# The attention phase of a three-layer kernel: the third group's output gate moves behind the fourth group's queries, keys and values

## What is computed

```python
def attention_mixer(h, positions, w_in, b_in, sinks, w_out, b_out):
    proj = h @ w_in + b_in
    q, k, v, z = jnp.split(proj, [ATTN_WIDTH, ATTN_WIDTH + KV_WIDTH, ATTN_WIDTH + 2 * KV_WIDTH], axis=-1)
    q = partial_rope(q.reshape(B, T, N_HEADS, HEAD_DIM), positions)
    k = partial_rope(k.reshape(B, T, N_KV_HEADS, HEAD_DIM), positions)
    o = sliding_window_gqa(q, k, v, sinks)
    return (o * jax.nn.silu(z)) @ w_out + b_out
```

## Time and profile before

| | us |
|---|---|
| median of three runs (3653.46 to 3659.43) | 3657.53 |
| the profiled execution: its time | 3661.34 |
| its span | 3660.0 |
| TensorE busy | 3461.1 (95%) |
| VectorE busy | 2063.2 (56%) |
| ScalarE busy | 1719.2 (47%) |
| GpSimd busy | 1353.8 (37%) |
| the attention phase, from the first unit's turn to its last product | 132.5 to 693.8 |

### The profile page before, as it was taken

How to read it: one execution, slowest core, us unless ns; L and a number is a source line. 1 busy time by engine, 2 the same in 40 slices (tenths; PEclk the granted TensorE clock), 3 DMA queues, 4 the chain that set the end, 5 groups by cost and what they waited for, 6 DMA issues and landing times. The chain is left out here.

```text
span 3660.0 us, 89296 instructions
## 1 busy us (share of the span) xinstructions
PE 3461.1 (95%) x37856; PEld 2777.6 (76%) x37856; DVE 2063.2 (56%) x4664; ACT 1719.2 (47%) x3161; POOL 1353.8 (37%) x1681
## 2 busy tenths in 40 slices
PE   8999998899899999999998989999999997999999
PEld 7888785688677777777776867777777775788777
DVE  4566766755555657555555445666666665343422
ACT  3455555522555556555554344444444442444422
POOL 5433321232455554555543333232322320444332
PEclk9999999999999999999998999999999998999999
DMA  4322211222110111111012341111111113322322
GB/s 136 90 67 81 61 53 33 84 98 94 34 44 25 42 30 36 36 30 42 24 42 87 133 142 43 42 43 43 43 43 38 42 37 112 86 70 70 104 81 92
DMA packets 252267, 231.66 MB, mean 63 GB/s; under 512 B 9120, under 2 KB 223072, under 8 KB 251872
## 3 DMA queue, kind: packets, MB, share of 16 engines
q1 hardware_dynamic: 251872, 225.94, 20.2%
HBM read 192.35 MB, written 33.55 MB: 62 GB/s over the span
## 5 line engine op out<-in xcount | busy, mean ns | idle before, releaser
L196 PE MATMUL bank<-hT_cut,arena_cut 128*128 128x512 f32 x2048 | 804.2, 393 | 0.0
L189 ACT ACTIVATE arena<-bank 128x512 f32<-128x512 f32 (+1 forms) x584 | 315.5, 569 | 560.3 <-PE bank L197 272.2
L195 PE MATMUL bank<-hT_cut,arena_cut 128*128 128x512 f32 x1240 | 552.1, 445 | 0.0
L197 PE MATMUL bank<-hT_cut,arena_cut 128*128 128x512 f32 x1240 | 488.2, 394 | 0.0
L195 PE MATMUL bank<-arena_cut,hT_cut 128*128 128x512 f32 (+1 forms) x1280 | 457.9, 358 | 30.3 <-DVE arena_cut L1153 25.7
L189 ACT ACTIVATE arena<-arena 128x512 f32<-128x512 f32 (+3 forms) x674 | 349.9, 554 | 261.7 <-POOL arena L1598 199.4
L196 PE MATMUL bank<-arena_cut,hT_cut 128*128 128x512 f32 (+1 forms) x1280 | 448.1, 350 | 0.0
L196 PEld LDWEIGHTS bank<-hT_cut,arena_cut 128*128 128x128 f32 x2048 | 387.4, 189 | 79.1 <-issue 18.6
L190 ACT ACTIVATE arena<-arena 128x256 f32<-128x256 f32 (+2 forms) x336 | 210.4, 627 | 412.5 <-DVE arena L179 187.9
L2848 POOL TENSOR_TENSOR arena_cut<-arena,arena_cut 128x256 fp32r<-128x256 f32 x272 | 218.0, 831 | 411.0 <-ACT arena_cut L189 411.0
L716 POOL TENSOR_TENSOR arena_cut<-arena,arena_cut 128x256 fp32r<-128x256 f32 x288 | 215.9, 777 | 414.2 <-ACT arena_cut L189 414.1
(11 more groups left out here) (267 smaller groups left out, 7129.7 us busy)
## 6 DMA issues: line engine op xcount, KB each, us to landing
arena<-in_w_in SPq DMA_DIRECT2D x100, 512.0 KB, 3.9
arena<-in_attn_w_in SPq DMA_DIRECT2D x144, 256.0 KB, 2.8
arena<-in_rec_w_in SPq DMA_DIRECT2D x62, 512.0 KB, 4.1
x_after<-arena SPq DMA_DIRECT2D x32, 512.0 KB, 2.6
arena<-x_after SPq DMA_DIRECT2D x32, 512.0 KB, 4.0
arena<-in_x SPq DMA_DIRECT2D x16, 512.0 KB, 3.6
h_after<-hT SPq DMA_DIRECT2D x4, 2048.0 KB, 7.8
hT<-h_after SPq DMA_DIRECT2D x4, 2048.0 KB, 16.5
```

What stands on the lines that cost most here:

```text
L189: return e.activation(out, a, f, bias=bias, scale=scale)
L195: pe.matmul(out, a[0], b[0], start=start, stop=False)
L196: pe.matmul(out, a[0], b[1], start=False, stop=False)
L197: return pe.matmul(out, a[1], b[0], start=False, stop=stop)
```

## The change

The fill's order is new: all nine blocks of groups 0 and 1, then the five row blocks of group 2, the five of group 3, the four gate blocks of group 2 and last the four of group 3. The table `due` is written anew for it. Group 2's gate now comes behind its outputs: they are copied to `oT`, and each gate piece, when it is there, is formed in `ub` and multiplied into the four tiles at once, in place. Group 2's halves stay in use for longer, one of them where the rows of group 3 were kept, so these rows move to the place of group 1's (`rows_1`), and they and the first two loads of the output projection wait for its release. The cut of group 3 moves two units earlier.

```diff
-    q_rows = [k.hT[:, :, cols(3)], rows_1, k.oT[:, :, cols(3)], k.hT[:, :, cols(0)]]
+    q_rows = [k.hT[:, :, cols(3)], rows_1, k.oT[:, :, cols(3)], rows_1]
...
-    block_of = lambda m: (m // blocks, m % blocks)
+    last_z = [(g, b) for g in (2, 3) for b in range(of_rows, blocks)]
+    order = [(g, b) for g in range(NG) for b in range(blocks) if (g, b) not in last_z] + last_z
+    block_of = lambda m: order[m]
...
-        if u < 32:
-            return 72 + (u + 1) * 9 // 2
-        if u < 43:
-            return 216 + (u - 31) * 40 // 11
-        return min(TICKS, 256 + (u - 42) * 32 // 19)
+        if u < 29:
+            return 72 + 4 * (u + 1)
+        if u < 44:
+            return 188 + (u - 28) * 36 // 15
+        return min(TICKS, 224 + (u - 43) * 64 // 20)
...
-            beside.setdefault(16 * (g - 2) + 11 + c // 2, []).append(("cut", g, c))
+            beside.setdefault(16 * (g - 2) + (11 if g == 2 else 9) + c // 2, []).append(("cut", g, c))
...
-            g, b, j = n // PAIRS, n % PAIRS // 4, n % 4
+            b, j = block_of(n // 4)[1], n % 4
...
+                if g == NG - 1 and b == 0 and i == 0:
+                    v.wait_ge(*Qpe.by("k", 7))
...
-            out = z_late[:, f, :] if g == NG - 1 else k.oT[:, f, cols(g)]
+            out = z_late[:, f, :] if g == NG - 1 else ub[n % 2] if g == 2 else k.oT[:, f, cols(g)]
...
+            if g == 2:
+                v.wait_ge(*z_v.by("o", n))
+                v.wait_ge(*o_v.by("o", 4 * (4 * g + 3) + f // 2))
+                v.tensor_tensor(k.oT[:, f, cols(g)], k.oT[:, f, cols(g)], ub[n % 2], ALU.mult).then_inc(*l_v.did("m"))
...
-            if t // 4 < NG - 1:
+            if t // 4 < 2:
...
+            elif t // 4 == 2:
+                v.wait_ge(*o_pe.by("o", u))
+                v.tensor_copy(out, bank).then_inc(*o_v.did("o"))
...
-    k.freed = [(c, Qpe.by("k", 7)) for c in range(2)] + [(c, f_pe.end()) for c in range(2, 5)]
+    k.freed = [(c, Qpe.by("k", NT - 1)) for c in range(2)] + [(c, f_pe.end()) for c in range(2, 5)]
```

## The result

| | median, us | runs | ratio to before (95% interval) |
|---|---|---|---|
| before | 3660.58 | 7 | |
| the change | 3670.68 | 7 | 1.0029 (1.0017 to 1.0040) |

The change made the kernel about 10 us slower, 0.29%. No change was forecast, at 3659.8 in a range of 3649 to 3669, so the forecast was wrong. The rival of the falling clock, at 0.23, came true. The profiled execution took 3672.95 (span 3671.6). So part of that closeness is luck.

A forecast was written before the change was run, and what follows sets the result against it. TensorE was taken to bound the attention phase, so its waits and low clock were summed: 11.0 + 6.8 + 24.2 + 0.5 = 42.5 us against 40.2 before. That +2.3 on the 3657.5 median gave 3659.8, range 3649 to 3669.

The forecast's parts named there:

- rival of the falling clock: Half clock follows all five or six long tail waits, plus GpSimd slowing: 11.6 us more, 3671.5; chance 0.23.
- I count two such falls over these units, 3.5: Units 43 to 63: two long TensorE waits are followed by half clock, costing 3.5 us.
- second rival: Falls to half clock at 1.5 to 2.6 us each; turns the verdict to slower from four falls on; chance 0.23.
- Units 0 to 28: Four ticks each; division waits 6.8 us, small waits unchanged at 4.2; together 11.0 against 11.0 before.
- Units 29 to 43: 36 ticks, no gate pieces; unit 32's wait and low clock go, bank and ScalarE waits come: 6.8 us against 6.5.
- Units 43 to 63: 64 ticks instead of 32, seven gate blocks; waits 20.7 us plus 3.5 of low clock, 24.2 against 22.7.
- scores, exponentials, tanh, piece, division: Within a unit: a gate piece ahead of the division, its tanh behind the exponentials, makes the unit 10.39 us long.
- The multiplies: Eight added on VectorE, 0.69 us each, 5.5 in all; they cost time only where ahead of a division.
- The junction: From last attention product to output projection: the 8.3 us stays, later weight loads add 0.5, bounds 0 and 4.
- The third rival: Start of output projection: its weights become the bound and move it by the whole 4 us, 3663.5; no chance given.
- The first rival: Behind unit 43 waits dissolve as ScalarE and VectorE get a unit ahead: 9 us instead of 24, 3645; chance 0.2.

The follow-up runs named there:

- tanh first: ScalarE's fill tanh put ahead of the unit's exponentials: 3634.5 us on the changed kernel (ratio 0.9930), 3634.2 on the kernel before (0.9936).
- division first: VectorE's division and, except at step 0, kept outputs put ahead of the unit's first two fill ticks: changed kernel 3634.9 us, kernel before 3639.5.
- both orders: Division and kept outputs ahead of the fill, plus tanh ahead of the exponentials: changed kernel 3630.7 us (0.9915), kernel before 3636.3 (0.9939).

## Why the prediction was wrong

- **The step that failed is "I count two such falls over these units, 3.5".** Five came behind unit 43, 9.0 us by the rows, and keeping TensorE busy gave back 5 (by the ratios) to 9 (in the profiled phase). The prediction's own rows said that two of three waits around 4 us were followed by half clock; with five or six such waits ahead, four was the number to count, and by the second rival's own price the verdict turned there. I took instead that "most of mine are shorter" would save them. It didn't: four waited 3.7 to 3.9, and the one that was clearly shorter, 2.51, was followed by half clock as well.
- **Term by term**: the sum had the waits 2.4 us longer than before, the clock 0.6 better, the junction 0.5. By the profiles it is 5.2, 7.9 worse, and 0.3. So 8.5 of the 11.1 us that the sum lacks are the clock's, 2.8 the waits'.
- **Units 0 to 28**: the waits for the division, 6.8 expected, are 6.7. But I left the small waits "as they are", 4.2, and they are 5.8: sums wait for ScalarE in units 15 (1.68, where it was 1.14), 19 (1.27) and 27 (1.41). And two waits of 2.3 us (units 12 and 16) were followed by half clock, which I had not priced at all; by the rows (3.8 x 0.35 and 3.8 x 0.44) 3.0 us.
- **Units 29 to 43**: 6.8 expected, 6.7 measured (5.1 and 1.6 in unit 43), with 1.6 in each of units 31, 35 and 43 as said. The wait of unit 32 and its fall went, as said.
- **Units 43 to 63**, waits alone: 20.7 expected; 21.9 without unit 43's. Unit 47 waited 3.9 in its two places together (4.3 expected), 49 3.9 (3.0), 52 3.9 (4.0), 54 and 55 2.2 (1.8), 57 3.9 (3.1), 59 3.7 (3.5). The chain "scores, exponentials, tanh, piece, division" was right, and the kernels with tanh first and division first each took away the link that they should. The stretch's busy time grew by 55.2 us where 44 were expected: about 7.5 of it is the clock, and the 32 added ticks took 1.5 each and not 1.4.
- **The multiplies**: 0.69 each expected, 0.84 measured, up to 1.1 beside GpSimd, as the Trainium skill's "SBUF — State Buffer" (Who interferes with whom) says of two SBUF inputs. The trace agrees: the multiply at 551.09 took 1.10, with GpSimd's subtractions running from 549.78 to 551.64. They cost 2.8 of waits, near what the sum had; the time without them does not differ beyond the noise.
- **The junction**: 0.5 expected, 0.3 measured. The third rival did not come.
- **The first rival** fell for the reason given: the tanh's lateness is fixed from the start of the unit. In unit 49 the piece started 7.39 us into the unit again (563.88 to 571.27), in unit 59 7.40. It is real, though, once the order inside the unit is changed.
- **"TensorE: Matmul & The Clock Gate" of the Trainium skill** (Why this matters for your kernels) had it that idle gaps between bursts bring half rate. The trace agrees for the seven waits of 2.2 us and more ahead of a turn here, of seven (one of 2.14, in unit 0, had full clock behind it); in the kernel before for two of four (3.72 and 4.32, but not 2.36 and 3.80).

What stays open: why a wait of 2.3 us is followed by half clock in one kernel and not in another (unit 16 before, 2.36, was not), and how much of the change's 10 us is the clock's, between 5 and 9. The spread from run to run (3653.5 to 3662.5 before, 3665.3 to 3673.8 after) goes with such falls at least in part: of the 69 executions of the kernel before that ran beside the experiments, the 24 with a mean granted clock of 0.984 or more took 3655.9 us in the mean, the 22 with 0.982 or less 3661.3. Where in the program the clock of these fell, no profile tells, since each shows one execution.

## What to carry to other kernels

Spreading fill over units does not remove a wait that one queue's order makes: look for what stands in front of the instruction that another engine waits for, and move that first; here one move (the division, or the tanh) took 18 to 23 us off the kernel before and 35 or 36 off the changed one, where the new order and table of the fill cost ten, or gave 6 to 9 with both moves made. When waits are summed, price what follows each as well as its length, at the rate at which the trace at hand shows it (two of three, not the hoped-for share). And test a suspected clock loss by filling the wait with idle products: it leaves every dependency alone. Then read the granted clock of all executions and not of the profiled one alone, and compare ratios to a kernel that ran beside each.

## What was not expected of the hardware

Waits of 2.3 us were followed by 3.4 us at half clock in two places of the changed kernel, and one of 1.66 us ahead of the turn of unit 50 in two variants of the kernel before (division first, where 0.62 more of idle followed inside the turn, and both orders). The same wait of 3.8 us in unit 53 was followed by full clock in one profile and by 6.8 us at half clock in another, with nothing near it changed. Eight filling products in waits of 2.5 to 3.9 kept the clock up in the changed kernel, with 2.10 us of idle left in the longest case; the same eight in waits of 3.7 and 4.3 of the kernel before, where 1.90 and 2.49 us of idle remained, did not, and thirteen did. So the length of the idle alone does not tell whether the clock falls.
